# Per-head sums of squares on TensorE with a block matrix of ones: nine two-column products or three 352-column ones

## The reference, cut to what matters

```python
def rms_norm(x, g):                      # x: (..., heads, 64)
    y = x * lax.rsqrt(jnp.mean(x * x, axis=-1, keepdims=True) + EPS)
    return y * g
...
h = rms_norm(x, g_attn)
proj = jnp.einsum('nld,de->nle', h, w_in)
qa, ka, va, qb, kb, vb = jnp.split(proj, SPLITS, axis=-1)
qa = rope_partial(rms_norm(heads(qa, 8), qn_a), pos)
ka = rope_partial(rms_norm(heads(ka, 8), kn_a), pos)
qb = rope_partial(rms_norm(heads(qb, 8), qn_b), pos)
kb = rope_partial(rms_norm(heads(kb, 2), kn_b), pos)
```

## Time and profile before

| | |
|---|---|
| median of 3 runs | 3116.52 us (3111.5 to 3117.1) |
| the profiled execution's own time | 3107.87 us |
| its span, first to last instruction | 3106.3 us |
| PE busy | 2876.3 us, 93% of the span |
| DVE busy | 1196.1 us, 39% |
| ACT busy | 828.0 us, 27% |
| POOL busy | 509.3 us, 16% |
| mean granted TensorE clock | 0.959 of full |

### The profile page before, as it was taken

How to read it: one execution, slowest core, us unless ns; L and a number is a source line. 1 busy time by engine, 2 the same in 40 slices (tenths; PEclk the granted TensorE clock), 3 DMA queues, 4 the chain that set the end, 5 groups by cost and what they waited for, 6 DMA issues and landing times.

```text
span 3106.3 us, 52475 instructions
## 1 busy us (share of the span) xinstructions
PE 2876.3 (93%) x19546; PEld 2659.6 (86%) x19546; DVE 1196.1 (39%) x2524; ACT 828.0 (27%) x1612; POOL 509.3 (16%) x211
## 2 busy tenths in 40 slices
PE   4999999977899999999969999997869999999998
PEld 4999666567899999999969996665859999999998
DVE  5444555452432222223254445554442222233223
ACT  2111566521221111112031126664122111112110
POOL 1222000022122122112122210001121221112110
PEclk6999999988899999999989999998879999999999
DMA  4121443124444445411021124521244455551111
GB/s 156 43 62 48 140 125 100 51 97 150 138 163 163 150 150 177 150 41 41 14 92 48 55 65 137 146 77 39 97 150 151 150 177 182 187 183 62 41 41 56
DMA packets 182634, 333.36 MB, mean 107 GB/s; under 512 B 30480, under 2 KB 142096, under 8 KB 179664
## 3 DMA queue, kind: packets, MB, share of 16 engines
q1 hardware_dynamic: 171632, 195.20, 20.2%
q0 software_dynamic: 2816, 135.99, 13.0%
q10 hardware_dynamic: 8032, 0.17, 0.2%
HBM read 309.08 MB, written 157.94 MB: 150 GB/s over the span
## 4 chain that ended last, share of the span: by engine, by line
PE 87%; DVE 5%; DMA 3%; issue 3%; ACT 2%; POOL 0%; ACTq 0%; DVEq 0%; SPq 0%; POOLq 0%
PE ps L404 66%; PE ps L1436 3%; PE ps L1450 3%; PE ps L1425 3%; DMA f_raw<-in_w_gate_up_dram 2%; PE ps L1346 2%; DVE g_lo L958 1%; PE ps L1499 1%; DVE hf L943 1%; PE ps L1356 1%; DVE hf L953 1%; PE ps L1487 1%; PE ps L1468 1%; DVE t_buf L943 1%; PE ps L1311 1%
## 5 line engine op out<-in xcount | busy, mean ns | idle before, releaser
L404 PE MATMUL ps<-g_hi,f_hi 128*128 128x352 f32 x2496 | 814.6, 326 | 35.1 <-DVE g_lo L958 35.0
L404 PE MATMUL ps<-g_hi,f_lo 128*128 128x352 f32 x2496 | 810.0, 325 | 0.0
L404 PE MATMUL ps<-g_lo,f_hi 128*128 128x352 f32 x2496 | 808.8, 324 | 0.0
L404 PEld LDWEIGHTS ps<-g_hi,f_hi 128*128 128x128 f32 x2496 | 473.7, 190 | 42.4 <-DVE g_lo L958 42.4
L630 POOL TENSOR_TENSOR f_lo<-f_raw,f_hi 128x2048 fp32r<-128x2048 f32 x66 | 303.6, 4611 | 1229.5 <-ACT f_hi L875 1229.5
L404 PEld LDWEIGHTS ps<-g_hi,f_lo 128*128 128x128 f32 x2496 | 474.7, 190 | 0.0
L404 PEld LDWEIGHTS ps<-g_lo,f_hi 128*128 128x128 f32 x2496 | 474.5, 190 | 0.0
L1269 DVE TENSOR_TENSOR silu<-silu,ps 128x352 f32<-128x352 f32 x132 | 68.8, 521 | 821.4 <-ACT silu L897 821.4
L1279 DVE TENSOR_TENSOR xm<-xm,ps 128x352 f32<-128x352 f32 x528 | 271.1, 520 | 199.4 <-PE ps L404 199.4
L404 PE MATMUL ps<-a_hi,f_hi 128*128 128x352 f32 x1056 | 340.6, 323 | 0.0
L404 PE MATMUL ps<-a_hi,f_lo 128*128 128x352 f32 x1056 | 338.4, 320 | 0.0
(11 more groups left out here) (166 smaller groups left out, 3396.3 us busy)
## 6 DMA issues: line engine op xcount, KB each, us to landing
out_dram<-in_cache_a_dram POOLq DMA_DIRECT2D x16, 8176.0 KB, 27.3
f_raw<-in_w_gate_up_dram SPq DMA_DIRECT2D x44, 1024.0 KB, 31.3
f_raw<-in_w_down_dram SPq DMA_DIRECT2D x22, 1024.0 KB, 4.9
k_near<-in_cache_a_dram SPq DMA_DIRECT2D x16, 1024.0 KB
v_near<-in_cache_a_dram SPq DMA_DIRECT2D x16, 1024.0 KB
w_raw<-in_w_in_dram SPq DMA_DIRECT2D x28, 512.0 KB, 3.9
k_far<-in_cache_a_dram SPq DMA_DIRECT2D x16, 768.0 KB
v_far<-in_cache_a_dram SPq DMA_DIRECT2D x16, 768.0 KB
```

The lines of the kernel that those rows point to most:

```text
L404: mm = pe.matmul(out, left(a, c), right(b, c), start=(start and c == 0 and k == 0), stop=(stop and c == n - 1 and k == 2))
```

## The change

`blocks` becomes a 128x128 matrix with ones in two 64x64 blocks, and it is now the stationary operand. The squares are the moving one, in three products of 352 columns. A column of squares then gives the head's sum on each of the head's 64 channels. `spread_heads` and the small tiles go; the root (ACT) and the reciprocal (DVE) are taken on all 128x1056 numbers, in `t_buf[1]`, from which the last DVE product reads.

```diff
-    c["c_blocks"] = np.kron(np.eye(2), np.ones((HD, 1))).astype(np.float32)
+    c["c_blocks"] = np.kron(np.eye(2), np.ones((HD, HD))).astype(np.float32)
...
-                def head_squares(unit, bank, n):
+                def head_squares(unit, bank, r):
                     act.wait_ge(projected.sem, projected.at(l, unit + 1))
-                    act.wait_ge(head_spread.sem, head_spread.at(l, n))
+                    act.wait_ge(rope.sem, rope.at(l, r))
                     nc.scalar.activation(pieces(t_buf[1][:, 0:T]), banks(bank), ACT.Square).then_inc(head_sq.sem, 1)
...
-                def roots_of_heads(n, r):
-                    act.wait_ge(rope.sem, rope.at(l, r + 7))
-                    for rows, a, b in ((P, 0, QT), (NS, QT, QT + 1)):
-                        nc.scalar.activation(
-                            t_buf[1][0:rows, a * P:b * P]...,
-                            head_means[0:rows, 1, 2 * a:2 * b]..., ACT.Sqrt).then_inc(head_root.sem, 1)
+                def roots_of_heads(n, bank):
+                    act.wait_ge(head_summed.sem, head_summed.at(l, n + 1))
+                    nc.scalar.activation(pieces(t_buf[1][:, 0:T]), banks(bank), ACT.Sqrt, scale=1.0 / HD,
+                                         bias=eps[:, 0:1]).then_inc(head_root.sem, 1)
...
-                    dve.wait_ge(head_summed.sem, head_summed.at(l, root + 1))
-                    for rows, a, b in ((P, 0, 2 * QT), (NS, 2 * QT, 2 * QT + 2)):
-                        nc.vector.tensor_scalar(head_means[0:rows, 0, a:b], ps[0:rows, bank, a:b], 1.0 / HD, EPS, ...
-                    for rows, a, b in ((P, 0, 2 * QT), (NS, 2 * QT, 2 * QT + 2)):
-                        nc.vector.reciprocal(head_means[0:rows, 1, a:b], head_means[0:rows, 0, a:b]).then_inc(rope.sem, 1)
                     nc.vector.tensor_tensor(t_buf[2][:], t_buf[2][:], sin[:], ALU.mult).then_inc(rope.sem, 1)
...
                     nc.vector.tensor_tensor(t_buf[0][:], t_buf[0][:], t_buf[2][:], ALU.add).then_inc(rope.sem, 1)
-                    dve.wait_ge(head_spread.sem, head_spread.at(l, root + 1))
+                    dve.wait_ge(head_root.sem, head_root.at(l, root + 1))
+                    nc.vector.reciprocal(t_buf[1][:, 0:T], t_buf[1][:, 0:T]).then_inc(rope.sem, 1)
...
-                    nc.vector.tensor_tensor(kt, t_buf[0][:], flat(0), ALU.mult).then_inc(rope.sem, 1)
+                    nc.vector.tensor_tensor(kt, t_buf[0][:], t_buf[1][:, 0:T], ALU.mult).then_inc(rope.sem, 1)
...
-                    for t in range(QT + 1):
-                        mm = pe.matmul(ps[0:rows_of(t), bank, 2 * t:2 * t + 2], t_buf[1][:, t * P:t * P + rows_of(t)],
-                                       blocks[:], start=True, stop=True)
+                    for c in range(NW):
+                        mm = pe.matmul(ps[:, bank + c, 0:W], blocks[:], t_buf[1][:, c * W:(c + 1) * W],
+                                       start=True, stop=True)
                     mm.then_inc(head_summed.sem, 1)
-
-                def spread_heads(bank, n):
...
                 for p in range(NP):
                     u, r, h = 2 + 4 * p, K_ROPE + ROPE_P * p, 1 + 3 * p
-                    pe.wait_ge(rope.sem, rope.at(l, r))
+                    pe.wait_ge(head_root.sem, head_root.at(l, h))
+                    project(u, 0, 0, (0,))
                     if p == 0:
+                        pe.wait_ge(rope.sem, rope.at(l, r))
                         turn(kt_all[:, 0, :], 2, k_turned)
-                    project(u, 0, 0, (0, 1))
+                    project(u, 0, 0, (1,))
...
+                    pe.wait_ge(head_root.sem, head_root.at(l, h + 1))
+                    project(u + 2, 0, 0, (0,))
                     pe.wait_ge(rope.sem, rope.at(l, r + K_ROPE))
                     turn(kt_all[:, 1 + p, :], 2, k_turned)
-                    project(u + 2, 0, 0, (0,))
                     sum_heads(3, h + 1, r + K_ROPE)
                     project(u + 2, 0, 0, (1,))
-                    spread_heads(3, h + 1)
...
-                    pe.wait_ge(rope.sem, rope.at(l, r + K_ROPE + Q_ROPE))
+                    pe.wait_ge(head_root.sem, head_root.at(l, h + 2))
                     project(u + 3, 1, 3, (0,))
                     sum_heads(0, h + 2, r + K_ROPE + Q_ROPE)
-                    project(u + 3, 1, 3, (1,))
-                    spread_heads(0, h + 2)
-                    project(u + 3, 1, 3, (2,))
+                    project(u + 3, 1, 3, (1, 2))
```

More of the change, by code:

```diff
@@ L133, in trunk @@
         ones = tensor(ctx, "ones", [P, 1])
-        blocks = tensor(ctx, "blocks", [P, 2])
+        blocks = tensor(ctx, "blocks", [P, P])
         cos = tensor(ctx, "cos", [P, T])
@@ L169, in trunk @@
         stage = tensor(pairs, "stage", [P, T])
-        head_means = tensor(pairs, "head_means", [P, 2, 2 * (QT + 1)])
         sq1, acc1, hf1 = [t_buf[0], t_buf[2]], t_buf[1], [kt_all[:, i, :] for i in range(2)]
@@ L259, in trunk @@
         projected = Signal("projected", UNITS)
-        K_ROPE, Q_ROPE = 10, 12
+        K_ROPE, Q_ROPE = 7, 9
         ROPE_P = K_ROPE + 2 * Q_ROPE
@@ L264, in trunk @@
         head_summed = Signal("head_summed", 1 + 3 * NP)
-        head_root = Signal("head_root", 2 * (1 + 3 * NP))
-        head_spread = Signal("head_spread", 1 + 3 * NP)
+        head_root = Signal("head_root", 1 + 3 * NP)
         v_staged = Signal("v_staged", 1 + NP)
@@ L740, in _ @@
                     u, r, h = 2 + 4 * p, K_ROPE + ROPE_P * p, 1 + 3 * p
-                    head_squares(u, 0, h)
-                    roots_of_heads(h, r)
-                    head_squares(u + 1, 3, h + 1)
+                    head_squares(u, 0, r)
+                    roots_of_heads(h, 0)
+                    head_squares(u + 1, 3, r + K_ROPE)
                     keep_k(p + 1, kv_rows[:, 0, p, :])
-                    roots_of_heads(h + 1, r + K_ROPE)
-                    head_squares(u + 2, 0, h + 2)
-                    roots_of_heads(h + 2, r + K_ROPE + Q_ROPE)
+                    roots_of_heads(h + 1, 3)
+                    head_squares(u + 2, 0, r + K_ROPE + Q_ROPE)
+                    roots_of_heads(h + 2, 0)
                     stage_v(u + 3, p + 1)
@@ L987, in roped @@
                     nc.vector.tensor_tensor(t_buf[0][:], t_buf[0][:], cos[:], ALU.mult).then_inc(rope.sem, 1)
[L988 to L994 removed]
                     nc.vector.tensor_tensor(t_buf[2][:], t_buf[2][:], sin[:], ALU.mult).then_inc(rope.sem, 1)
[L996 removed]
+                    dve.wait_ge(rope.sem, rope.at(l, r + 4))
                     nc.vector.tensor_tensor(t_buf[0][:], t_buf[0][:], t_buf[2][:], ALU.add).then_inc(rope.sem, 1)
[L998 to L999 removed]
+                    dve.wait_ge(head_root.sem, head_root.at(l, root + 1))
+                    nc.vector.reciprocal(t_buf[1][:, 0:T], t_buf[1][:, 0:T]).then_inc(rope.sem, 1)
+                    dve.wait_ge(rope.sem, rope.at(l, r + 6))
                 def k_rope(unit, gain, r, root, kt):
                     roped(unit, 0, gain, r, root)
[L1003 removed]
+                    nc.vector.tensor_tensor(kt, t_buf[0][:], t_buf[1][:, 0:T], ALU.mult).then_inc(rope.sem, 1)
                 def q_rope(unit, bank, gain, r, root, q, rows):
                     roped(unit, bank, gain, r, root)
[L1008 removed]
+                    nc.vector.scalar_tensor_tensor(q, t_buf[0][:, 0:SEQ], -1.0, t_buf[1][:, 0:SEQ],
                                                    ALU.mult, ALU.mult).then_inc(rope.sem, 1)
@@ L1013, in q_rope @@
                                                        t_buf[0][half, SEQ:T].rearrange("p (b t) -> p b t", t=TS), -1.0,
-                                                       flat(bank)[half, SEQ:T].rearrange("p (b t) -> p b t", t=TS),
+                                                       t_buf[1][half, SEQ:T].rearrange("p (b t) -> p b t", t=TS),
                                                        ALU.mult, ALU.mult).then_inc(rope.sem, 1)
@@ L1379, in _ @@
                 sum_heads(0, 0, 0)
[L1380 to L1382 removed]
+                project(1, 1, 3, (1, 2))
                 for p in range(NP):
                     u, r, h = 2 + 4 * p, K_ROPE + ROPE_P * p, 1 + 3 * p
[L1385 removed]
+                    pe.wait_ge(head_root.sem, head_root.at(l, h))
+                    project(u, 0, 0, (0,))
                     if p == 0:
+                        pe.wait_ge(rope.sem, rope.at(l, r))
                         turn(kt_all[:, 0, :], 2, k_turned)
[L1388 removed]
+                    project(u, 0, 0, (1,))
                     pe.wait_ge(v_staged.sem, v_staged.at(l, p + 1))
```

11 lines of the change are left out of this document (removed).

## The result

The changed kernel takes 3138.61 us (median of 4 runs, 3137.3 to 3144.7) against 3115.06 us (4 runs) of the kernel before: ratio 1.0081, 95% interval 1.0063 to 1.0098, 23.5 us slower. The forecast was 3124.4 us, 7.9 slower, with a range of 3109 to 3136. Slower was right, the size was not.

What follows compares the result with a forecast made beforehand. PE was taken to bound the projection before the change. Stage changes of -1.2 us, clock falls in the pairs +7.5 and at attention's start +1.6 gave +7.9 on 3116.52: 3124.4 us, range 3109 to 3136.

Steps and rivals of the forecast that it cites:

- The sum on PE: Projection, PE: six float32 instructions of 352 columns take 1.77 us, against 1.83 before.
- The reciprocal: Projection, DVE: the new reciprocal over 1056 columns takes 6.75 us, at 6.25 ns per element.
- the cheap: Rival: DVE's reciprocal is cheaper on long rows, 5.65 us, total 3095.5 us; chance 0.08.
- the dear one: Rival: DVE's reciprocal costs 9.0 us, total about 3167 us; chance 0.05.
- the dear sum: Rival: PE's sum costs its whole durations, 3.05 us, total 3132 us; chance 0.08.
- The mechanism: Projection pairs: DVE's unit chain of 16.04 us makes PE wait 2.8 us before the third sum, 4 before the scores.
- For a query the end is 1.22 and two small ones: DVE, end of a query unit's chain: last product 1.22 us, with two small ones 1.55 us.
- 0 to 1.5, I take 0.8, twice: Start of attention: the clock falls after PE's 4 us wait, costing 0.8 us twice, 1.6 in all.
- the clock in the pairs: Projection pairs: waits of 2.8 us lower PE's clock, five falls of 1.5 us, 7.5 us in all.
- The rival in which the clock holds: Rival: PE's clock does not fall after the 2.8 us waits, total 3115.3 us, no change; chance 0.27.
- It just fits: First turn of the values: 4.9 us of projection covers 4.70 us of turn, store and copy; uncovered, 1 or 2 a layer.
- The end of the stage: Before the first scores: PE waits 4 us for DVE's last unit, 3.3 us lost a layer.

Runs made afterwards that it cites:

- Experiments 1: Changed kernel without the large reciprocal; the last product multiplies queries and keys by the root instead: 3078.53 us, ratio 0.9890 to the kernel before.
- experiments 2: Changed kernel with the third sum of each pair one third of the value unit later on PE: 3104.22 us, ratio 0.9970 to the kernel before.
- experiment 4: Changed kernel with 24 unneeded PE matmuls ahead of the third sum in all pairs but the last: 3129.04 us, ratio 1.0048 to the kernel before.
- Experiment 3: Changed kernel with POOL's split of the next pair's key weights waiting until DVE is through with queries a: 3130.61 us, ratio 1.0047 to the kernel before.
- experiment 5: Changed kernel with unneeded PE matmuls ahead of the last pair's third sum and before the first scores: 3130.71 us, ratio 1.0055 to the kernel before.
- experiment 6: Changed kernel with the first pair's turn of the values one third later on PE: 3137.71 us, ratio 1.0073 to the kernel before.

## Why the prediction was wrong, point by point

- **The sum on PE** (1.77 us) was right, as the chain of the changed kernel shows (start, us, engine, tile, line, matmuls):

```profile
81.60 1.77 PE ps L1335 x6
```

- **The reciprocal** (6.75 us) was right to 5 ns (26 with a mean of 6745 ns), and with it the rivals that hung on its price, the cheap and the dear one, are out, as is the dear sum.
- **The mechanism** was right: one unit's chain of 16 us, the wait ahead of the third sum, the wait before the first scores. Experiments 1 and 2 show it from both sides.
- **Failed: "For a query the end is 1.22 and two small ones"**, the term of the last product. Its duration was read where it reads PSUM and POOL is idle; the change moves that input to SBUF and, by the longer chain, moves the product over POOL's subtraction. There the product of the queries a took 2.80 to 2.87. With hand-overs 0.4 shorter than worked out the third sum came 1.2 us later than forecast, six times, 7.1 us. From that sum to the next pair's first one it took 25.8 us where the forecast has 22.2 + 3.84, so that with the clock held a pair is 58.0 us (experiment 4) and not 57.0. Experiment 3 gives 8.0 back.
- **Failed: the clock at attention's start, "0 to 1.5, I take 0.8, twice".** Measured 4.0 and 4.7 (experiment 5: all of it the clock). The price was taken from a dense stretch, where the clock is back after 3.4 us; at attention's start it stayed at 0.50 for 13.7 and 17.1 us. PE is less dense there (11.05 of 13.38 us busy in the kernel before), but that this is the reason was not tested. This error is as large as the one before it, 8.7 us measured against 1.6.
- **Partly failed: the clock in the pairs.** That it falls was right. I took five falls of 1.5; it fell in all six, three times for 6.8 us instead of 3.4, and that is 12.9 us in the two profiles instead of 7.5. The rival in which the clock holds is out.
- **Failed: "It just fits" at the first turn.** The store of the keys landed in 3.5 us instead of 1.6. The load of the next weights (2 x 256 KB, issued at 96.05) and the store (issued at 96.79) now meet, where before the store was issued at 94.20 and the load at 96.51; that the load slows the store is argued from this order, and no run moved it. So 1.7 us of wait a layer stand there. The bound "1 or 2 us a layer" had it, the value taken did not.
- **The end of the stage** was 3.3 a layer and measured 2.4: in the last pair no key weights follow, POOL is idle, and the hand-overs are shorter.

The four parts of the table sum to 28.4 us where the forecast has 7.9 (31.7 with its last line); the medians say 23.5. What of the rest belongs to the single falls of the clock in attention is argued from two profiles, not shown.

## What to carry to other kernels

When a step on all channels takes the place of one on a few numbers, work out the latency of the whole chain through the shared buffer and lay it against the order of the engine that sets the time: here 6.75 us three times in a row turned a gain of 34.7 us into a loss of 23.5, and moving one small step by 3.8 us on PE gave 34 back. Price a wait of PE with what the clock does behind it, and take that price from rows of the stretch that follows, not from another one. And when an operand moves from PSUM to SBUF, or an instruction moves in time, look up what POOL does at that moment.

## What the runs showed of the hardware

- A reciprocal of 128x1056 float32 on DVE took 6.745 us, 6.25 ns an element, the slope between 16 and 32 elements of the trace before.
- A DVE product with two SBUF inputs that began during POOL's subtraction took 2.8 instead of 1.22 us and ended 1.07 to 1.08 us after it, six times of six; where DVE began first, its product kept its time and POOL's subtraction took up to 3.3 instead of 2.4. DVE instructions with one input in PSUM kept their time (0.52 us over POOL's work).
- Single waits of PE of 3.98 to 4.03 us among dense matmuls were followed by a granted clock of 0.5 (1.2 GHz) in all six pairs, for 3.4 or 6.8 us. Behind waits of 2.33 to 2.45 us it fell in 11 of 14 cases (the changed kernel 1 of 2, experiment 3 7 of 8, experiment 4 1 of 2, experiment 6 2 of 2), for 3.4 us. At the start of attention, behind waits of 2.1 to 6.4 us, it stayed there for 10.2 to 17.1 us in the changed kernel and experiments 2, 3, 4 and 6. Matmuls that nobody needs, put into the wait, kept it at 1.00.
